# Attention scores of a stick-breaking layer: from zero-padded queries to two row tiles of 64

## The reference, cut to what matters

```python
z = einsum('bqhd,bkhd->bhqk', q, k) * SB_HEAD_DIM ** -0.5        # 16 heads of 64
visible = k_pos[None, :] < q_pos[:, None]
log_keep = where(visible, log_sigmoid(-z), 0)
suffix = (reverse cumsum of log_keep over keys, exclusive)
weights = where(visible, exp(log_sigmoid(z) + suffix), 0)
out = einsum('bhqk,bkhd->bqhd', weights, v)
```

## Time and profile before

| What | us |
|---|---|
| Median of 3 runs (915.58 to 916.60) | 916.16 |
| Span of the profiled execution, first to last instruction | 914.5 |
| TensorE busy in it | 804.0 |
| VectorE busy | 561.4 |
| ScalarE busy | 405.1 |
| GpSimd busy | 92.6 |

### The profile page before, as it was taken

The page is one execution under the profiler, slowest core; times in us unless marked ns, Lnnn a source line. Parts: engine busy times, 40 slices in busy tenths (PEclk is TensorE's granted clock), DMA queues, the critical chain, the costliest instruction groups (busy, mean ns, idle before and its releaser), DMA issues.

```text
span 914.5 us, 12496 instructions
## 1 busy us (share of the span) xinstructions
PE 804.0 (88%) x3920; PEld 571.7 (63%) x3921; DVE 561.4 (61%) x722; ACT 405.1 (44%) x449; POOL 92.6 (10%) x160
## 2 busy tenths in 40 slices
PE   2799999999999999469980599999999999999983
PEld 0476777878687787248850466666666666666641
DVE  1466475655557473763668566776676677667647
ACT  5225454545535452651322245444555544455513
POOL 3000211112021111130004000000000000000124
PEclk9999999999999999699995699999999999999997
DMA  8918385583939473500018994966999999999363
GB/s 320 350 48 257 91 284 161 212 240 133 329 93 323 111 261 102 226 27 1 1 57 307 342 400 179 332 242 229 350 365 367 358 370 366 373 365 369 123 233 145
DMA packets 130196, 215.86 MB, mean 236 GB/s; under 512 B 4666, under 2 KB 55930, under 8 KB 130179
## 3 DMA queue, kind: packets, MB, share of 16 engines
q1 hardware_dynamic: 127300, 205.17, 64.4%
q0 software_dynamic: 2880, 10.49, 3.1%
HBM read 195.72 MB, written 45.09 MB: 263 GB/s over the span
## 4 chain that ended last, share of the span: by engine, by line
PE 78%; DVE 8%; DMA 7%; SPq 2%; issue 2%; POOL 2%; ACT 1%; POOLq 0%; DVEq 0%; ACTq 0%
PE z L782 41%; PE fill_ps L1425 18%; PE z L1425 13%; DMA ada_w<-in_ada_w 2%; DMA x_slot<-slots_in 2%; PE fill_ps L1342 2%; DMA exp_w<-in_exp_w_down 1%; PE fill_ps L912 1%; DVE exp_w L766 1%; PE fill_ps L1348 1%; SPq L962 1%; PE z L883 1%; POOL slots_in L477 1%; DVE hid L742 1%; DVE h_T L1188 1%
## 5 line engine op out<-in xcount | busy, mean ns | idle before, releaser
L446 DVE TENSOR_TENSOR w_lo<-exp_w,w_hi 128x1024 fp32r<-128x1024 f32 x148 | 173.0, 1220 | 64.9 <-ACT w_hi L442 63.0
L442 ACT ACTIVATE w_hi<-exp_w 128x1024 fp32r (+1 forms) x148 | 154.7, 1058 | 65.4 <-PE z L782 49.3
L782 PE MATMUL z<-exp_w,hidT 128*128 x288 | 128.3, 598 | 2.1
L782 PE MATMUL z<-w_hi,x_slotT_hi 128*128 128x512 f32 x288 | 121.6, 422 | 2.5 <-DVE x_slotT_lo L717 2.5
L782 PE MATMUL z<-w_hi,x_slotT_lo 128*128 128x512 f32 x288 | 114.7, 398 | 0.0
L782 PE MATMUL z<-w_lo,x_slotT_hi 128*128 128x512 f32 x288 | 113.7, 395 | 0.0
L782 PEld LDWEIGHTS z<-exp_w,hidT 128*128 128x128 f32 x288 | 53.2, 190 | 66.6 <-issue 66.6
L553 ACT ACTIVATE y_slot<-z 128x1024 f32<-128x1024 f32 x18 | 18.5, 1026 | 141.7 <-PE z L782 141.7
L1425 PE MATMUL fill_ps<-h_hi,wp_hi 128*128 128x512 f32 x192 | 77.0, 401 | 2.4 <-DVE h_lo L1194 2.4
L1425 PE MATMUL fill_ps<-h_lo,wp_hi 128*128 128x512 f32 x192 | 76.6, 399 | 0.0
L1425 PE MATMUL fill_ps<-h_hi,wp_lo 128*128 128x512 f32 x192 | 76.2, 397 | 0.0
(11 more groups left out here) (272 smaller groups left out, 1337.8 us busy)
## 6 DMA issues: line engine op xcount, KB each, us to landing
exp_w<-in_exp_w_gate SPq DMA_DIRECT2D x20, 2048.0 KB
exp_w<-in_exp_w_up SPq DMA_DIRECT2D x20, 2048.0 KB
exp_w<-in_exp_w_down SPq DMA_DIRECT2D x20, 2048.0 KB
ada_w<-in_ada_w SPq DMA_DIRECT2D x12, 2048.0 KB, 9.0
slots_in<-zeros SPq DMA_DIRECT2D x7, 2048.0 KB, 12.8
w_pair<-in_sb_w_qkv SPq DMA_DIRECT2D x24, 512.0 KB, 5.3
x_slot<-slots_in SPq DMA_DIRECT2D x20, 512.0 KB, 11.5
slots_out<-y_slot SPq DMA_DIRECT2D x18, 512.0 KB, 4.4
```

The source lines that it names most:

```text
L442: act.activation(w_hi[:, u % RING, :].unsqueeze(1), raw_unit(b, u), ACT.Copy).then_inc(hi_ready, 1)
L446: dve.tensor_tensor(w_lo[:, u % RING, :].unsqueeze(1), raw_unit(b, u), w_hi[:, u % RING, :].bitcast(F32).unsqueeze(1), ALU.subtract).then_ ...
L782: return pe.matmul(out, lhsT, rhs, start=start, stop=stop, skip_group_check=True)
```

## The change

Queries are kept without padding in `q_T[128, 640]`, head 0 on partitions 0 to 63 and head 1 on 64 to 127. A score matmul takes 64 partitions of the keys and of the queries, and the two heads alternate, always into two different banks. The banks are laid out anew: 4 + h holds for head h the scores of key block 2 (256 columns), of the running streams among themselves (128) and against their cached keys (128). The masks, sums and `values` follow that layout.

```diff
-    q_z = sb("q_z", [P, 2, TOK], c=phase_a)
+    q_T = sb("q_T", [P, TOK], c=phase_a)
...
-        pool.memset(q_z[:, :, :], 0.0).then_inc(consts_set, 1)
...
-            for first, step, n in (((0, 512, 3), (1408, 512, 1)), ((1536, 384, 2), (2048, 256, 2), (2560, 128, 2)))[half]:
+            for first, step, n in (((0, 512, 3), (1408, 512, 1)), ((1536, 384, 2), (2048, 256, 4)))[half]:
...
-                dve.tensor_scalar(q_z[0:HD, 0, 0:SEQ], src[0:HD, :], SCALE, None, ALU.mult)
-                ins = dve.tensor_scalar(q_z[HD:P, 1, 0:SEQ], src[HD:P, :], SCALE, None, ALU.mult)
+                ins = dve.tensor_scalar(q_T[:, 0:SEQ], src, SCALE, None, ALU.mult)
...
-                dve.tensor_scalar(q_z[0:HD, 0, SEQ:TOK], src[0:HD, 0:P], SCALE, None, ALU.mult)
-                dve.tensor_scalar(q_z[HD:P, 1, SEQ:TOK], src[HD:P, 0:P], SCALE, None, ALU.mult)
+                dve.tensor_scalar(q_T[:, SEQ:TOK], src[:, 0:P], SCALE, None, ALU.mult)
...
-            def late(h):
-                acc(zb(2 + h, 0, 384), k_T[:, P:2 * P], q_z[:, h, P:SEQ], start=True)
-                return acc(zb(2 + h, 384, 512), k_T[:, 3 * P:4 * P], q_z[:, h, 3 * P:SEQ])
-            for h in range(2):
-                acc(zb(h), k_T[:, 0:P], q_z[:, h, 0:SEQ], start=True)
-            late(0).then_inc(z_ready, 1)
-            late(1)
-            acc(zb(4), k_T[:, 2 * P:3 * P], q_z[:, :, 2 * P:SEQ], start=True)
-            acc(zb(5, 0, 256), k_T[:, SEQ:TOK], q_z[:, :, SEQ:TOK], start=True)
-            past = zb(5, 256, 512).rearrange("p (h s q) -> p h s q", h=2, s=NS)
-            for s in range(NS):
-                mm = acc(past[:, :, s, :], past_kT[:, s, :], q_z[:, :, SEQ + SS * s:SEQ + SS * (s + 1)])
+            def score(h, bank, a, k, queries, start):
+
+                d = slice(HD * h, HD * h + HD)
+                n = queries.stop - queries.start
+                return acc(zb(bank + h, a, a + n), k[d], q_T[d, queries], start=start)
+
+            for h in range(2):
+                score(h, 0, 0, k_T[:, 0:P], slice(0, SEQ), True)
+            for h in range(2):
+                score(h, 2, 0, k_T[:, P:2 * P], slice(P, SEQ), True)
+            for h in range(2):
+                mm = score(h, 2, 384, k_T[:, 3 * P:4 * P], slice(3 * P, SEQ), False)
+            mm.then_inc(z_ready, 1)
+            for h in range(2):
+                score(h, 4, 0, k_T[:, 2 * P:3 * P], slice(2 * P, SEQ), True)
+            for h in range(2):
+                score(h, 4, 256, k_T[:, SEQ:TOK], slice(SEQ, TOK), False)
+            for s in range(NS):
+                for h in range(2):
+                    mm = score(h, 4, 384 + SS * s, past_kT[:, s, :], slice(SEQ + SS * s, SEQ + SS * (s + 1)), False)
             mm.then_inc(z_ready, 1)
...
             for sp in (sp_hi, sp_lo):
-                acc(blocks_of(z, 2048 + P, 256, 2), nones_r[:, :], blocks_of(sp, 1408, 512, 2))
-                acc(zb(5, 256, 512), nones_r[:, :], sp[:, 2560:2816])
+                for h in range(2):
+                    acc(two_of(z, 2048 + 512 * h + P, PAST_AT - 2048 - P), nones_r[:, :],
+                        two_of(sp, 1408 + 512 * h, SELF - 1408))
```

More of the change, by code:

```diff
@@ L122, in build @@
     ZH = ZC // 2
+    SELF = 2048 + 256
+    PAST_AT = SELF + P
     ew_at = next_place()
@@ L240, in blocks_of, with two_of @@
         return buf[:, lo:lo + step * n].rearrange("p (n c) -> p n c", c=step)[:, :, first % step:first % step + P]
+    def two_of(buf, first, step):
+        return bass.AP(tensor=buf, offset=first, ap=[[ZC, P], [step, 2], [1, P]])
     ada_v = io["ada_w"].rearrange("o (k p) n -> p (o k) n", p=P)
@@ L1021, in _ @@
         pool.memset(zeros[:, :], 0.0).then_inc(consts_set, 1)
-        pool.memset(q_z[:, :, :], 0.0).then_inc(consts_set, 1)
         pool.memset(c_T[:, :, :], 0.0).then_inc(consts_set, 1)
-        pool.wait_ge(consts_set, 9)
+        pool.wait_ge(consts_set, 8)
         pool.affine_select(out=ident[:, :], in_=ident[:, :], compare_op=ALU.not_equal, fill=1.0, base=0,
@@ L1030, in _ @@
         for g in range(NG4):
-            pool.wait_ge(consts_set, 11 + 3 * g)
+            pool.wait_ge(consts_set, 10 + 3 * g)
             pool.affine_select(out=sum_sel[:, :], in_=sum_sel[:, :], compare_op=ALU.not_equal, fill=1.0,
@@ L1039, in _ @@
                                channel_multiplier=1).then_inc(consts_set, 1)
-        pool.wait_ge(consts_set, 11 + 3 * NG4)
+        pool.wait_ge(consts_set, 10 + 3 * NG4)
         pool.affine_select(out=sel_tok[:, :, :], in_=sel_tok[:, :, :], compare_op=ALU.not_equal, fill=1.0,
@@ L1060, in mask @@
             pool.nop(nofuse=True)
-            v = buf[:, 2560:2816].rearrange("p (a s q) -> p a s q", a=2, s=NS)
+            v = blocks_of(buf, SELF, 512, 2).rearrange("p a (s q) -> p a s q", s=NS)
             pool.affine_select(out=v, in_=v, compare_op=ALU.is_ge, fill=0.0, base=0,
@@ L1079, in _ @@
             act.wait_ge(sq_ready, t + 1)
-        act.wait_ge(consts_set, 9)
+        act.wait_ge(consts_set, 8)
         act.activation(rstd[:, :], rstd[:, :], ACT.Sqrt, scale=1.0 / D, bias=eps1[:, 0:1]).then_inc(std_ready, 1)
@@ L1112, in attend @@
                 act.activation(sp_hi[:, a], ew_sp[:, a], ACT.Copy).then_inc(sp_hi_ready, 1)
-            act.activation(sums_hi[:, :, 0:P], blocks_of(ew_sp, 2048, 256, 2), ACT.Copy).then_inc(sums_hi_ready, 1)
+            act.activation(sums_hi[:, :, 0:P], blocks_of(ew_sp, 2048, 512, 2), ACT.Copy).then_inc(sums_hi_ready, 1)
             act.wait_ge(sums_ready, 3 * p + 3)
@@ L1155, in _ @@
         dve.wait_ge(setup_T, 1)
-        dve.wait_ge(consts_set, 9)
+        dve.wait_ge(consts_set, 8)
         dve.tensor_copy(c_T[:, :, 0:NC], fill_ps[:, 0, 0:KD * NC].rearrange("p (k c) -> p k c", c=NC)).then_inc(setup_T_used, 1)
@@ L1159, in _ @@
         dve.tensor_copy(norm_gT[:, :], fill_ps[:, 0, 128 + 6 * KD:128 + 8 * KD]).then_inc(setup_T_used, 1)
-        dve.wait_ge(consts_set, 11)
+        dve.wait_ge(consts_set, 10)
         dve.tensor_copy(ntri_r[:, :], ntri[:, :]).then_inc(tri_ready, 1)
@@ L1279, in attend @@
             dve.wait_ge(sp_masked, 3 * p + 3)
-            dve.tensor_tensor(last_q, blocks_of(ew_sp, 2048 + P, 256, 2), blocks_of(ew_sp, 1408, 512, 2),
+            dve.tensor_tensor(last_q, blocks_of(ew_sp, 2048 + P, 512, 2), blocks_of(ew_sp, 1408, 512, 2),
                               ALU.add).then_inc(sums_ready, 1)
-            dve.tensor_tensor(two_q[:, :, 0:P], blocks_of(ew_sp, 1024 + P, 512, 2), blocks_of(ew_sp, 2048, 256, 2),
+            dve.tensor_tensor(two_q[:, :, 0:P], blocks_of(ew_sp, 1024 + P, 512, 2), blocks_of(ew_sp, 2048, 512, 2),
                               ALU.add).then_inc(sums_ready, 1)
@@ L1290, in attend @@
             dve.wait_ge(sums_hi_ready, 2 * p + 1)
-            dve.tensor_tensor(sums_lo[:, :, 0:P], blocks_of(ew_sp, 2048, 256, 2), sums_hi[:, :, 0:P].bitcast(F32),
+            dve.tensor_tensor(sums_lo[:, :, 0:P], blocks_of(ew_sp, 2048, 512, 2), sums_hi[:, :, 0:P].bitcast(F32),
                               ALU.subtract).then_inc(sums_lo_ready, 1)
@@ L1326, in _ @@
         split_w(1)
-        dve.wait_ge(consts_set, 12 + 3 * NG4)
+        dve.wait_ge(consts_set, 11 + 3 * NG4)
         dve.tensor_copy(sel_tok_r[:, :, :], sel_tok[:, :, :]).then_inc(sel_ready, 1)
@@ L1349, in transposes @@
             return mm
-        pe.wait_ge(consts_set, 12 + 3 * NG4)
+        pe.wait_ge(consts_set, 11 + 3 * NG4)
         pe.wait_ge(c_loaded, 80)
@@ L1471, in values @@
                 for h in range(2):
-                    src = (512 * h, 1024 + 512 * h, 2048 + 256 * h, 1408 + 512 * h)[kb]
+                    src = (512 * h, 1024 + 512 * h, 2048 + 512 * h, 1408 + 512 * h)[kb]
                     n = SEQ - kb * P
@@ L1477, in values @@
                 acc(z[HD * h:HD * h + HD, 512:640], v_tok[:, NTP, HD * h:HD * h + HD],
-                    ew_w[:, 2560 + P * h:2688 + P * h], start=True)
+                    ew_w[:, SELF + 512 * h:SELF + 512 * h + P], start=True)
             for s in range(NS):
                 for h in range(2):
-                    c = 2816 + P * h + SS * s
+                    c = PAST_AT + 512 * h + SS * s
                     mm = acc(z[HD * h:HD * h + HD, 512 + SS * s:512 + SS * (s + 1)],
```

## The result

The changed kernel takes 899.84 us, the median of 4 runs (899.07 to 900.78); the kernel before takes 916.38 beside it (915.58 to 916.75). The ratio is 0.9819, with an interval of 0.9805 to 0.9833: 16.5 us less.

A forecast was written before the change was run, and what follows sets the result against it. TensorE's own work was taken to set the pace in the loop's pairs. 7 x 2.33 us, 1.2 for the last pair and 0.3 ahead of the first make 17.8 us off 916.16: 898.4 us, range 894 to 907.

The forecast's parts named there:

- The overlap of row tiles: Scores, products with `k_T`: two heads in row tiles run at once, 2.42 us in place of 4.85.
- The assumption taken over from the column tiles: Scores: row tiles overlap as the column tiles of `values` did, where two heads ran at once in 2.42 us.
- The loads of two tiles at once: Scores, cached keys: 32 weight loads in place of 16, two tiles loading together, 1.70 us as before.
- loads in turn: Rival, scores: row tiles stream at once but load one after the other, 3.40 us for cached keys; 913.3 us, chance 0.08.
- The switch: Ahead of and behind the scores: one more change of array tiling per pair, taken as 0.10 us.
- The gain per pair: Scores of each pair: 4.22 us in place of 6.55, a gain of 2.33 us.
- The chain: Elementwise work between scores and sums: moves earlier with the projections, leaving 0.6 us of slack before bank 3.
- the chain takes over: Rival, loop pairs: elementwise work moves only 0.75 us, so 1.44 us per pair remain; 904.6 us, chance 0.12.
- The first pair: Scores of the first pair: the same 2.33 us gained, plus 0.3 us from a copy dropped ahead of it.
- The low-clock stretch that was to stay: First pair's scores: 3.41 us of their 8.27 run at half the clock, and this was expected to remain.
- The last pair: Uncovered last pair: 0.7 us from an earlier `ew_sp` and some 0.5 from second-half selects, together 1.2 us.

The follow-up runs named there:

- Experiment 4: Changed kernel with zero-padded queries and all 128 rows again, keeping the new bank layout and alternating order: 939.47 us, ratio 1.0264 to the kernel before.
- Experiment 1: Changed kernel with all score matmuls of head 0 and then all of head 1 in each half, not alternating: 925.58 us, ratio 1.0119 to the kernel before.
- Experiment 2: Changed kernel with only the cached-key products put head by head, those with `k_T` still alternating: 919.77 us, ratio 1.0051 to the kernel before.
- experiment 5: Changed kernel with cached-key products cut over columns too, four tiles of 64x64: 897.98 us, ratio 0.9804 to the kernel before.
- experiment 10: The changed kernel again, unedited, on the same chip as the run with three edits together: 899.97 us, ratio 0.9815 to the kernel before.

## Why the prediction was right

**The overlap of row tiles: right.** The assumption taken over from the column tiles held: 2.48 us for 2.42 forecast. Experiment 4 shows that the layout and the order carry none of it without the tiles. Experiment 1 shows that the tiles need an order in which the two heads stay close, though not strict alternation. That neighbours also always write different banks was never varied.

**The loads of two tiles at once: right.** 1.79 us for 1.70. Experiment 2 makes "loads in turn" for the cached keys and shows the price, 1.36 us in the scores of a pair where the rival had 1.70, and as much again in the projection behind, which the rival did not have. That the time of a load goes by columns and not by rows, the rule of the Trainium skill ("TensorE: Matmul & The Clock Gate", section "LDWEIGHTS (loading the stationary operand)"), agrees with the traces from both sides. In turn, a load of 128 columns comes every 0.112 us with 64 rows (experiment 2) and with 128 (experiment 4). Two tiles at once do two loads of 128 columns in 0.112 us, and four tiles do four of 64 columns in 0.064 (1.02 / 16).

**The switch: 0.02 us for 0.10.** Ahead of the scores nothing is to be seen: from the first matmul of the values to the first of the next scores it is 7.31 us before and after. The first matmul behind the scores stands 0.335 us ahead of the next, where it was 0.314 before. The scores came to 4.27 us for 4.22 because the three errors, 0.06 and 0.09 too little and 0.10 too much, nearly cancel.

**The gain per pair: 2.19 us, not 2.33.** From start to start, as the prediction counts, the scores gave 6.55 - 4.27 = 2.28. (The chain's pieces, 6.64 and 4.27, run to the modelled end of the last matmul.) The projection behind them gave 0.1 back: from its first matmul to the first of the sums it takes 16.74 and 16.90 us in turn, where it took 16.72, at the full clock both times. The prediction had no such term. What makes the difference wasn't tried.

**The chain: right.** 0.51 us of slack for 0.6 forecast, with the steps as worked out: `sp_lo`, mask and `ew_sp` moved with the projections. The rival "the chain takes over" was as near as the text said: experiment 5 needed 0.64 us more to reach it.

**The first pair: 2.73 us for 2.33, by luck.** Two things were left out, and they offset each other. The low-clock stretch that was to stay did not come in this execution, so the scores lie at the full clock and gain 3.84 us from start to start (8.11 to 4.27). And VectorE takes |z| there only at 77.29, behind weight splits that wait for the first transfers of `w_pair`, so that TensorE stands once:

```profile
94.96 0.50 PE L1429 MATMUL z<-sp_hi,ntri_r 128*128 128x512 f32 x1 [0.62 <-DVE sp_lo L1292]
```

From the sums' first matmul to the values' it is 11.15 us there for 10.23 before, which takes 0.9 back; the projection takes 0.2. These 2.73 us and six times 2.19 make 15.9 from the first pair's scores to the last's, where 7 x 2.33 = 16.3 was forecast; the scores of the first pair begin 0.4 us earlier (71.62 for 72.00), where 0.3 was.

**The last pair: its steps came, and the low clock took them back.** 1.2 us was forecast, and from the last scores to the end it is 555.2 us before and 555.3 after. `ew_sp` comes 0.6 us earlier against the scores. The modulation slice ran at the low clock, which the working had priced at 0.25 in place of 1.13:

```profile
351.03 3.64 PE L1346 MATMUL fill_ps<-ada_w,c_T 128*32 128x512 f32 x16 [3.64 <-DMA ada_w<-in_ada_w]
```

3.64 us for 2.62. The second `sp_lo` and the values, in the chain of the kernel before:

```profile
380.56 1.77 DVE sp_lo L1288
...
392.94 5.04 PE z L1425 x52
```

and of the changed one:

```profile
363.40 1.77 DVE sp_lo L1292
...
375.63 5.55 PE z L1429 x52
```

Counted from the last scores (359.29 before, 343.05 after) the `sp_lo` comes 0.9 us earlier and the values 1.1, nearly the 1.2 forecast. The values then take 0.5 us longer, and in phase B the rest goes. The windows of the low-clock stretches from the modulation slice on (columns as above):

```profile
349.07:369.55 20.48, 10.88 (x37) 6.29 (x37) 13.35 (x16) 14.68 (x15) 3.60 (x5) 0.50 0.69 259
372.96:379.79 6.83, 4.16 (x16) 1.75 (x18) 5.70 (x9) 6.83 (x14) 1.91 (x4) 0.50 0.00 0
454.88:458.29 3.41, 3.41 (x21) 1.99 (x18) 2.48 (x3) 0.28 (x1) 0.00 (x0) 0.50 0.00 0
```

The second covers the values. The last has TensorE busy throughout, and the kernel before has none there: ahead of it the output projection of phase B still begins 0.6 us earlier against the last scores (391.06 for 407.94), and behind it the same matmuls come some 0.9 us later. In the profile of experiment 10, the same kernel, the end takes 552.3 us, but there the first scores start at 73.44 and not at 71.62. So single profiles of this kernel differ by 2 to 3 us at either end, and what a term of 1 us in the last pair is worth in the end can't be read from one of them. The medians say that 1.3 us of the 17.8 did not come; in the two profiles it is 1.6, 0.4 of it from the first scores to the last and the rest behind them.

## What to carry to other kernels

When heads of 64 rows share the array, write their matmuls so that neighbours in the program lie in different row tiles. Here the streams and the loads of two tiles then ran at once (2.48 us for 4.85, two loads in 0.112 us). Overlap reached only three records ahead of the program, so short runs of one head kept most of it and runs of 16 loads nearly none. Where loads pace the products, cut columns: four loads of 64 columns went in 0.064 us, while a load of 64 rows took the 0.112 us of one of 128. And before taking more out of TensorE, measure the slack of the chain behind it: here it was 0.5 us, and a second saving paid in full only once that chain had been started earlier.

## What the runs showed that was not expected

In experiments 2 and 4 the projection behind the scores ran some 1.4 us longer in most loop pairs although TensorE had not been idle in the scores ahead of it: around the end of 3.2 and 3.5 us of short products paced by loads in turn, the granted clock fell to 0.50 (1.2 GHz) for 3.41 us. In the changed kernel, where these products take 1.79 us, no pair of the loop shows such a stretch. In the kernel before, with 1.70, only the first does, and there it begins with the scores. Order on TensorE thus cost twice, once in the scores and once, about as much, in the work behind them. That it is these products which bring the clock down is inferred from their place ahead of the stretches, and not all of it fits: two loop pairs of experiment 4 and one of experiment 2 have no stretch, nor have five of the seven in experiment 1, where the cached keys also come in turn. No run separated these products from other causes.
